# A hybrid decoder layer: half of the mixer's output product with 7 block products in place of 8 on four weight pieces

## The reference, cut to what matters

```python
merged = jax.nn.sigmoid(gate_mla) * o_mla + jax.nn.sigmoid(gate_lru) * o_lru
x = x + rmsnorm(merged @ w_out[l], g_post_mix[l])     # the product that the change touches
h = rmsnorm(x, g_pre_x[l])
mn = rmsnorm(mem, g_mem[l])
cq = (h @ w_cq[l]).reshape(b, s, X_HEADS, X_HEAD_DIM)   # needs x
ck = (mn @ w_ck[l]).reshape(b, m, X_HEADS, X_HEAD_DIM)  # does not need x
```

## Time and profile before

| | |
|---|---|
| median of 3 runs | 1707.48 us |
| the profiled execution, whole | 1706.93 us |
| its span, first to last instruction | 1705.1 us |
| granted TensorE clock, mean | 0.999 |
| PE busy | 1696.3 us (99%) |
| DVE, ACT, POOL busy | 1269.6, 969.0, 255.1 us |

### The profile page before, as it was taken

The page is one execution under the profiler, slowest core; times in us unless marked ns, Lnnn a source line. Parts: engine busy times, 40 slices in busy tenths (PEclk is TensorE's granted clock), DMA queues, the critical chain, the costliest instruction groups (busy, mean ns, idle before and its releaser), DMA issues.

```text
span 1705.1 us, 24572 instructions
## 1 busy us (share of the span) xinstructions
PE 1696.3 (99%) x8899; PEld 1456.1 (85%) x8899; DVE 1269.6 (74%) x1598; ACT 969.0 (57%) x1225; POOL 255.1 (15%) x324
## 2 busy tenths in 40 slices
PE   9999999999999999999999999999999999999998
PEld 8888888888888888888888888888888888888887
DVE  7766675468788897676557687778877778977797
ACT  6656655454577765454446575556555555545554
POOL 0012212210245430002121101110001110001100
PEclk9999999999999999999999999999999999999999
DMA  9644459997555648499998855556765556765555
GB/s 345 204 132 152 152 189 287 320 266 228 166 184 174 187 169 291 143 362 282 308 260 249 229 198 191 182 186 220 238 200 178 183 196 208 238 201 192 197 185 204
DMA packets 228440, 369.81 MB, mean 217 GB/s; under 512 B 8336, under 2 KB 164624, under 8 KB 226320
## 3 DMA queue, kind: packets, MB, share of 16 engines
q1 hardware_dynamic: 210352, 325.61, 56.4%
q0 software_dynamic: 12096, 28.32, 8.6%
q10 hardware_dynamic: 5920, 14.94, 2.3%
HBM read 364.64 MB, written 32.51 MB: 233 GB/s over the span
## 4 chain that ended last, share of the span: by engine, by line
PE 97%; DVE 1%; ACT 1%; issue 1%; POOL 0%; DMA 0%; SPq 0%; DVEq 0%; ACTq 0%; POOLq 0%
PE ps L606 48%; PE ps L681 31%; PE ps L928 7%; PE ps L620 3%; PE ps L773 2%; PE ps L911 1%; PE ps L837 1%; PE ps L743 1%; ACT wsp L1559 0%; PE ps L713 0%; PE ps L866 0%; PE ps L842 0%; PE ps L732 0%; PE ps L1271 0%; PE ps L652 0%
## 5 line engine op out<-in xcount | busy, mean ns | idle before, releaser
L1901 DVE TENSOR_TENSOR wsp<-raw,wsp 128x2048 fp32r<-128x2048 f32 (+2 forms) x304 | 673.8, 2229 | 215.7 <-ACT wsp L1336 199.7
L1336 ACT ACTIVATE wsp<-raw 128x2048 fp32r<-128x2048 f32 (+2 forms) x278 | 509.7, 1843 | 160.6 <-PE ps L681 129.3
L606 PE MATMUL ps<-asp,wsp 128*128 128x512 f32 x3032 | 529.0, 336 | 0.0
L606 PEld LDWEIGHTS ps<-asp,wsp 128*128 128x128 f32 x3032 | 463.8, 188 | 62.4 <-issue 0.2
L681 PE MATMUL ps<-wsp,hsp 128*128 128x512 f32 x1632 | 375.4, 390 | 0.0
L681 PEld LDWEIGHTS ps<-wsp,hsp 128*128 128x128 f32 x1632 | 305.7, 188 | 63.3
L606 PE MATMUL ps<-hsp,wsp 128*128 128x512 f32 (+1 forms) x1744 | 314.0, 339 | 0.0
L606 PEld LDWEIGHTS ps<-hsp,wsp 128*128 128x128 f32 x1744 | 268.3, 188 | 36.5
L681 PE MATMUL ps<-wsp,asp 128*128 128x512 f32 x768 | 175.1, 390 | 0.0
L1347 ACT ACTIVATE cr<-ps 128x256 f32<-128x256 f32 x185 | 69.2, 380 | 183.8 <-PE ps L606 166.4
L681 PEld LDWEIGHTS ps<-wsp,asp 128*128 128x128 f32 x768 | 144.0, 188 | 29.8
(11 more groups left out here) (315 smaller groups left out, 1474.6 us busy)
## 6 DMA issues: line engine op xcount, KB each, us to landing
raw<-in_w_up SPq DMA_DIRECT2D x88, 1024.0 KB, 5.2
raw<-in_w_in SPq DMA_DIRECT2D x56, 1024.0 KB, 5.3
raw<-in_w_in SPq DMA_DIRECT2D x32, 768.0 KB, 4.4
raw<-in_w_down SPq DMA_DIRECT2D x24, 1024.0 KB, 5.6
sums<-in_w_down POOLq DMA_DIRECT2D x76, 256.0 KB, 7.7
raw<-in_w_o_mla SPq DMA_DIRECT2D x16, 1024.0 KB, 10.5
raw<-in_w_o_lru SPq DMA_DIRECT2D x16, 1024.0 KB, 5.9
raw<-in_w_out SPq DMA_DIRECT2D x16, 1024.0 KB, 10.3
```

Source lines behind the costliest of these rows:

```text
L606: mm = pe.matmul(ps[:, bank, 0:w], lhs(part, k), x[:, 0:w], start=(f and part == 0), stop=(l and part == 1))
L1336: act.activation(wsp[:, p0 % SLOTS, 0, 0:n], raw[:, p0 % SLOTS, 0:n], ACT.Copy).then_inc(hi_done, 1)
L1901: dve.tensor_tensor(wsp[:, slot, 1, 0:n], raw[:, slot, 0:n], wsp[:, slot, 0, 0:n].bitcast(F32), ALU.subtract).then_inc(lo_done, 1)
```

## The change

Pieces 8 to 15 of PH_WO become twelve pieces: three plain ones (row pairs 0, 1, 2), then first and made for row pairs 4, 5, 6 and 7 in a row, then the plain piece of row pair 3. PH_WO has 20 pieces. The four activation sums of each of the pairs 4 to 7 are made in the first half, from banks 4 to 7: ACT copies a bank (`wo_copy`), DVE makes four sums of 128 columns (`wo_form_sums`), ACT and DVE split them (`wo_form_high`, `wo_form_low`). POOL makes four more weight sums, in two batches of two, when the first half of PH_GL is done; the batches for `w_down` start where they did. At the end DVE combines banks 0 to 3 (`wo_products`) and adds the plain banks 4 to 7 (`wo_plain`), both ahead of `lo` of PH_CK's third piece; squares and gains of the second half read the sums in SBUF. PE's wait ahead of PH_CK is now for `wo_products`; the wait for the first half's gains moves to the first of the "first" pieces. The last plain piece runs bank by bank. The core of the diff (left out: names of semaphores and tiles, `x_mm`, and the shift of an index in the last phases):

```diff
+WO_PLAN = [("plain", pair) for pair in range(8)] + [
+    ("plain", 0), ("plain", 1), ("plain", 2), ("first", 4), ("made", 4), ("first", 5), ("made", 5),
+    ("first", 6), ("made", 6), ("first", 7), ("made", 7), ("plain", 3)]
...
-for _n in (2, 0, 1):
+for _n in (2, None, 0, 1):
+    if _n is None:
+        WO_SUMS = len(SUMS)
+        SUMS += [(1024, 2 * WO_PLAN[c][1]) for c in WO_MADE]
+        continue
...
-PH_WO = Phase(PH_OL[-1], 4, [0] * 4)
+PH_WO = Phase(PH_OL[-1], 1, [0] * len(WO_PLAN), twice=WO_FIRST)
...
+            for c, (kind, pair) in enumerate(WO_PLAN):
+                k, c0 = 2 * pair, (c // 8 > 0) * 1024
+                if kind == "plain":
+                    piece(PH_WO, 0, c, 2, 1024, w_out[:, k:k + 2, c0:c0 + 1024])
+                elif kind == "first":
+                    first_blocks(PH_WO, c, w_out, k, c0)
+                else:
+                    made_sums(PH_WO, c, wo_sum(c))
...
+                arrive(PH_WO, 0, c)
+                if c < 8:
+                    pe.wait_ge(m_lo, 2 * c + 2)
+                if c == 8:
+                    pe.wait_ge(h_scaled, KT // 2 + 4)
+                if c == WO_FIRST[0]:
+                    pe.wait_ge(wo_gain, 4)
+                if kind == "first":
+                    pe.wait_ge(h_form_lo, wo_forms + pair - 4 + 1)
...
+                elif c == len(WO_PLAN) - 1:
+                    for m in range(2):
+                        for b in range(2):
+                            for k in (k0, k1):
+                                mm = x_mm(k, m, b, last=(k == k1))
+                            if (m, b) != (1, 1):
+                                mm.then_inc(wo_mm, 1)
+                elif kind == "plain":
+                    for k in (k0, k1):
+                        for m in range(2):
+                            for b in range(2):
+                                mm = x_mm(k, m, b, first=(c == 8 and k == k0))
+                elif kind == "first":
+                    form_mm(q1, block(k0, 0), slot, 1, c == WO_FIRST[0], c == WO_FIRST[-1])
+                    form_mm(dn_plain_bank(1, 0, 1), block(k1, 0), slot, 3, False, False)
+                    mm = form_mm(dn_plain_bank(1, 0, 0), form(3), slot, 2, False, False)
+                else:
+                    first, last = c == WO_MADE[0], c == WO_MADE[-1]
+                    form_mm(q5, form(1), slot, 0, first, last)
+                    form_mm(q7, form(0), slot, 1, first, last)
+                    form_mm(q6, form(2), slot, 2, first, last)
+                    mm = form_mm(dn_plain_bank(1, 1, 1), block(k1, 1), slot, 3, False, False)
                 mm.then_inc(gemm_step, 1)
...
-            pe.wait_ge(wo_gain, 4)
+            pe.wait_ge(gl_out, 16 + 4)
...
+                    if n < 4:
+                        wo_ready(act, n)
                     m, b = n // 2 % 2, 2 * (n // 4) + n % 2
+                    if n == 0:
+                        act.wait_ge(h_form_raw, wo_forms + 4)
                     if n >= 2:
                         act.wait_ge(wo_sq, n - 1)
-                    square(junk[n % 2], ps[:, n, :], 0, m, b).then_inc(wo_sq, 1)
+                    if n >= 4:
+                        act.wait_ge(gl_out, 16 + n + 1)
+                    square(junk[n % 2], wo_res(n) if n >= 4 else ps[:, n, :], 0, m, b).then_inc(wo_sq, 1)
...
+            def wo_copy(n):
+                act.wait_ge(merged_out, 8)
+                act.wait_ge(m_lo, 8 + 2 * n + 2)
+                if n >= 2:
+                    act.wait_ge(h_form_raw, wo_forms + n - 1)
+                act.activation(HT[n % 2], ps[:, 4 + n, :].rearrange("p (k t) -> p k t", k=2), ACT.Copy).then_inc(h_scaled, 1)
+            def wo_form_high(n):
+                act.wait_ge(h_form_raw, wo_forms + n + 1)
+                if n == 2:
+                    act.wait_ge(mem_lo, KT)
+                act.activation(WO_FORMS[n][:, :, 0, :], WO_RAW.rearrange("p (f t) -> p f t", f=4), ACT.Copy).then_inc(h_form_hi, 1)
...
+            for c in range(LEAD, len(WO_PLAN) + LEAD):
+                if c in WO_FIRST:
+                    first_high(PH_WO, c)
+                elif c in WO_MADE:
+                    made_high(PH_WO, c, GL_SUMS + WO_MADE.index(c))
+                else:
+                    hi(PH_WO, 0, c)
+                p = c - LEAD
                 if p in (1, 2):
                     merged_hi(range(4 + 4 * p, 8 + 4 * p))
                 if p == 2:
                     act.wait_ge(merged_out, 8)
                     act.dma_start(g_res, a["g_post_mix"].to_broadcast([P, D])).then_inc(g_mix_in, 16)
                 if p == 3:
+                    wo_copy(0)
                     act.wait_ge(mem_cols_in, 16)
                     act.wait_ge(gemm_step, PH_OL[1].g_end)
                     mem_high(range(8))
-                if p == 6:
-                    mem_high(range(8, KT))
+                    wo_copy(1)
                 if p == 4:
                     act.wait_ge(m_lo, KT)
                     act.dma_start(a_tok, x_tok).then_inc(x2_in, 16)
+                    wo_form_high(0)
+                    wo_copy(2)
+                    mem_high(range(8, KT))
+                if p == 5:
+                    wo_form_high(1)
+                    wo_copy(3)
+                if p == 6:
+                    wo_form_high(2)
+                if p == 7:
+                    wo_form_high(3)
                 if p == 8:
                     wo_square(range(4))
+                if c == WO_MADE[-1] + 2:
+                    act.wait_ge(gemm_step, PH_WO.g(0, PH_WO.used[WO_MADE[-1]]))
+                    act.activation(wo_res(1), ps[:, 0, :], ACT.Copy).then_inc(gl_q1, 1)
...
+            def wo_form_sums(n):
+                two = HT[n % 2]
+                f7_f5, f6, f3 = (WO_RAW[:, a * P:b * P] for a, b in ((0, 2), (2, 3), (3, 4)))
+                dve.wait_ge(h_scaled, KT // 2 + n + 1)
+                dve.wait_ge(h_form_lo, wo_forms + n)
+                own.mark(dve.tensor_tensor(f7_f5[:, 0:P], two[:, 0, 0:P], two[:, 0, P:2 * P], ALU.subtract))
+                own.link(dve.tensor_tensor(f7_f5[:, P:2 * P], two[:, 0, P:2 * P], two[:, 1, P:2 * P], ALU.subtract))
+                own.link(dve.tensor_tensor(f6, WO_RAW[:, P:2 * P], two[:, 0, 0:P], ALU.subtract))
+                dve.tensor_tensor(f3, f6, two[:, 1, 0:P], ALU.add).then_inc(h_form_raw, 1)
+            def wo_form_low(n):
+                dve.wait_ge(h_form_hi, wo_forms + n + 1)
+                f = WO_FORMS[n]
+                dve.tensor_tensor(f[:, :, 1, :], WO_RAW.rearrange("p (f t) -> p f t", f=4), f[:, :, 0, :].bitcast(F32),
+                                  ALU.subtract).then_inc(h_form_lo, 1)
+            def wo_products():
+                q6, q7, q5 = (ps[:, b, :] for b in (1, 2, 3))
+                dve.wait_ge(gemm_step, PH_WO.g(0, PH_WO.used[WO_MADE[-1]]))
+                dve.wait_ge(gl_q1, 3)
+                dve.tensor_tensor(WO_V, wo_res(1), q6, ALU.add).then_inc(gl_out, 1)
+                dve.wait_ge(gl_out, 16 + 1)
+                dve.tensor_tensor(wo_res(3), WO_V, q7, ALU.add).then_inc(gl_out, 1)
+                dve.tensor_tensor(wo_res(0), q5, WO_V, ALU.subtract).then_inc(gl_out, 1)
+                dve.wait_ge(gl_out, 16 + 2)
+                dve.tensor_tensor(wo_res(2), q5, wo_res(3), ALU.subtract).then_inc(gl_out, 1)
+            def wo_plain():
+                dve.wait_ge(gl_out, 16 + 4)
+                for n in range(4, 8):
+                    wo_ready(dve, n)
+                    dve.tensor_tensor(wo_res(n), wo_res(n), ps[:, n, :], ALU.add).then_inc(gl_out, 1)
             def make_diag(norm, m):
                 dve.tensor_scalar(diag[m], ident[:, :], nst[:, norm, 14 + m:15 + m], None, ALU.mult).then_inc(diag_made, 1)
-            for p in range(16):
-                lo(PH_WO, p // 4, p % 4 + LEAD)
+            for c in range(LEAD, len(WO_PLAN) + LEAD):
+                if c in WO_FIRST:
+                    sums_rest(PH_WO, c)
+                    first_low(PH_WO, c)
+                else:
+                    lo(PH_WO, 0, c)
+                p = c - LEAD
                 if p in (1, 2):
                     merged_lo(range(4 + 4 * p, 8 + 4 * p))
                 if p == 3:
+                    wo_form_sums(0)
                     mem_low(range(8))
+                if p == 4:
+                    wo_form_low(0)
+                    wo_form_sums(1)
+                    mem_low(range(8, KT))
+                if p == 5:
+                    wo_form_low(1)
+                    wo_form_sums(2)
                 if p == 6:
-                    mem_low(range(8, KT))
+                    wo_form_low(2)
+                    wo_form_sums(3)
+                if p == 7:
+                    wo_form_low(3)
                 if p == 8:
                     dve.wait_ge(g_mix_in, 16)
                     dve.wait_ge(mem_lo, KT)
                     wo_gains(range(4))
+                if c == WO_MADE[-1] + 2:
+                    wo_products()
+            wo_plain()
...
```

(50 more changed lines are left out.)

24 lines of the change are left out of this document (15 added, 9 removed).

## The result

The changed kernel takes 1710.64 us (median of 7 executions, 1710.25 to 1714.19) against 1707.44 us for the kernel before on the same chip. The medians are 3.2 us apart and the means 4.5 us (1711.94 against 1707.43), because three of the seven executions lie above 1713; the ratio, which weighs all executions, is 1.0027, interval 1.0018 to 1.0036: slower. The forecast was 1709.8 us. The profiled execution took 1714.18 us (span 1712.2), 7.25 us more than the one of before, so its waits are those of a bad execution, not of the median.

The account below looks back on a forecast made before the run. PE, busy 99% of the span, was taken to bound the kernel. -2.72 + 0.2 + 2.9 + 1.9 = +2.3 us on the profiled 1706.93 gave 1709.2, and 0.55 for the median 1709.8 us; range 1705.9 to 1714.3.

Parts of the forecast that it names:

- The matmuls, -2.72 us: PH_WO: four pairs of 21 matmuls replace four pieces of 24, so 12 x 226.7 ns go, all that can be won.
- First half, the new batches of POOL, mem: PH_WO's first half, POOL's added weight sums from about 656 us, and mem's tiles two steps earlier: each costs 0.
- The row: Four pairs in PH_WO at DVE's 5.69 us pitch just keep up with PE; 0.2 us added, but the lead goes.
- Landings of 19 and 20, +2.9 us: Last PH_WO piece and first PH_CK piece: loads take 10.3 us where 7.4 is allowed; ends 0 and +6.0.
- wait forecast ahead of PH_CK: Profile sign: PE waits before PH_CK, released by DVE's product additions, with ACT's `hi` of 20 held by DMA before it.
- Behind the product, +1.9 us: After PE enters PH_CK, DVE's longer queue starts gains 2.9 us later against 1.4 slack, plus 0.4 at the fifth tile.
- burst: Loads behind the pairs meet POOL's copies, 13.4 us for piece 20: +5.4 us, 1712.9; chance 0.34 together with stalls between pairs.
- quiet case: Pieces 19 and 20 land within 7.3 us: -0.8 us, or -2.1 with the short chain, 1706.7 us; chance 0.26.
- a stall of 2.5: Sums of made pieces take over 5.7 us to land, DVE waits in each pair: +2.5 us; shares chance 0.34.

Follow-up runs that it names:

- control: The kernel before the change with POOL's last four w_down batches moved later, as in the changed kernel's own such run: 1720.17 us, ratio 1.0079.
- second profile: The changed kernel itself, unaltered, run once more: median 1711.66 us, the profiled execution 1709.82 us.
- row early: Changed kernel with its four pairs right behind the first plain piece, three plain pieces after them, gains and squares ahead of piece 22's split: 1710.36 us, ratio 1.0020.
- split early row: Changed kernel with pairs starting behind the first plain piece, one plain piece between second and third pair, gains and squares ahead of piece 22's split: 1708.00 us.
- spread row: Changed kernel with its third plain piece moved between the second and the third pair: 1708.82 us, ratio 1.0009.

## Why the prediction was right, and where its sum was not

- *The matmuls, -2.72 us: right.* With POOL's copies out of the way the stretch is 2.71 us shorter than its control.
- *First half, the new batches of POOL, mem: right at 0.* No wait of PE in the first half or up to piece 18, and none new in PH_GL.
- *The row: right.* `lo` of 14, 16 and 18 were forecast for 852.4, 858.1 and 863.9 and were done 0.2 to 0.3 us later, at the forecast pitch; PE lost nothing inside it.
- *Landings of 19 and 20, +2.9 us: right in kind.* 10.3 us was assumed; 9.4 and 9.6 came, and PE waited 2.0 us; in the second profile 4.9 and 9.7, and 2.2 us. The wait forecast ahead of PH_CK, released by DVE's product additions, came in the second profile; in the first it fell on piece 19. With POOL's copies out of the way the same loads took 5.0 to 7.1 us. The rule that was weighed is from the Trainium skill's "DMA: Bandwidth & Descriptors", section "Queues, rings and completion order": each engine serves its queues in turn, a packet at a time. These landings, 5.0 to 7.1 us against 9.4 to 15.6, fit it; that the engines take turns packet by packet, no run here shows.
- *Behind the product, +1.9 us: the step that failed.* It counted DVE's extra operations ahead of the gains, but took pieces 21 and 22 as landed. They were loaded into POOL's four copies and took 15 us, so the gains started 10.3 us after PE entered PH_CK (875.02 to 885.33), not 7.1, and the wait was 4.3 us in the first profile. The "burst" that was priced for piece 20 struck here. In the second profile, where piece 21 landed in 11.8 us and PE itself came 2.2 us later to PH_CK, it was 0.6.
- *What a wait of PE does to its clock was not priced at all*: 1.75 us in the first profile, about 1.6 in the second (64 matmuls in 12.90 us in the view by time, 11.28 before).
- *Two slips in the rivals' sums.* The quiet case's -2.1 leaves out the row's 0.2, and a stall of 2.5 on top of the burst's +5.4 makes +7.9 in full, not +6.8. Neither moves the forecast.

For the first profile the terms are 2.0 (piece 19) + 0.1 (head of PH_CK) + 0.7 (first 64 matmuls of PH_CK, 11.8 us) + 4.3 (before x's transposes) + 0.4 (transposes at DVE's pace) + 1.75 (clock) = 9.25, less 2.72 is 6.5. The chains agree: from the start of the stretch to the query product (the 128 matmuls behind the second transposes) they have 907.83 - 799.42 = 108.41 us and, before, 900.94 - 799.07 = 101.87. The executions differ by 7.25 us; of the 0.7 that is left, 0.35 lies ahead of the stretch and 0.2 behind it. The forecast's +2.3 came close to the median's +3.2 because it stands between executions that lose less behind the product and such as lose much more; the means are 4.5 apart. That was in part luck, a fit of the sum and not of each term.

## What to carry to other kernels

A faster form that makes PE need less time than the loads and splits behind it uses up the line's lead; price the first ordinary pieces behind it, and the work that stands in order behind their loads, by the landing under the background traffic of that moment, piece by piece and not once. Break such a row with ordinary work, end it some pieces before the phase does, and put what others wait for ahead of what waits for a load. Moving the background copies away moves the collision with them: look first whether the loads at the new place have a lead to lose. And where PE will wait, add what its clock may lose afterwards.

## What the runs showed of the hardware that was not expected

Waits of PE of 4.0, 2.2 and 3.6 us (changed kernel, its second profile, row early) were each followed by some 4 us in which the granted clock read 0.50 to 0.74, near the lower level; the first cost 1.75 us, the second about 1.6, the third 18.25 - 16.3 = 1.9. A wait of 2.2 us at the head of PH_CK in the split early row, and that of 2.0 us for piece 19, were followed by no fall. Nor was one of 2.4 us before x's transposes in the spread row followed by one (clock 1.00 from 886 to 894), at the place where the changed kernel's clock fell; but one of 1.9 us in the control, ending at 1245.84, was followed by 0.50 from 1248 to 1250. So the length of a wait does not by itself say whether the clock falls.

The same loads of 1 MB (piece 19 and `w_ck`) landed in 5.0 to 7.1 us without POOL's copies and in 9.4 to 15.6 us beside them (first profile of the changed kernel), with nothing else changed in the program. Moved, the same copies stretched the loads of `w_down` from 5.7 to 11.7 us, and both programs lost over 10 us there.
